# Rebuilding a state-space mixer: split f32r products of 128 columns between the chunk cores, and wider modulation strips

## The reference, cut to what matters

```
proj = h @ w_in                      # 1024 x (q k v f u_pool z xbc dt gates)
y_att  = forgetting_attention(q, k, v, log_sigmoid(f + b)) @ w_attn_o      # 16 heads of 64
y_pool = multiscale_pool(u_pool) by 4 windows, then 4 group products
# state-space branch: 4 groups of 8 heads of 64, state 128
xbc = silu(causal_depthwise_conv(xbc, 4 taps) + b);  xs, B, C = split(xbc)
dt = softplus(dt_raw + dt_bias);  a_cs = cumsum over the chunk of dt * -exp(a_log)
scores = (C B^T) * exp(a_cs[l] - a_cs[s]) * dt[s]  where l >= s
states = sum of B * exp(a_cs[end] - a_cs) * dt * xs, carried from chunk to chunk with exp(a_cs[end])
y = scores @ xs + (C @ states before the chunk) * exp(a_cs) + d_skip * xs
y = rms_norm_per_group(y * silu(z)) * norm_w;   y_ssm = y @ w_o
mix = (sigmoid(g0) * y_att + sigmoid(g1) * y_pool + sigmoid(g2) * y_ssm) @ w_out
```

## Time and profile before

| | us |
|---|---|
| median of 3 runs (3609.61 to 3610.5) | 3609.9 |
| profiled execution, its own time | 3614.2 |
| its span from first to last instruction | 3612.5 |
| TensorE busy | 2898.8 (80%) |
| VectorE busy | 1620.5 (45%) |
| ScalarE busy | 912.7 (25%) |
| mean granted TensorE clock | 0.877 of full speed |

### The profile page before, as it was taken

One profiled execution on the slowest core, in us unless ns is written; L12 is line 12 of the kernel. 1 busy time (PEld: TensorE's weight loads), 2 busy tenths in 40 slices (PEclk: granted clock), 3 DMA queues, 4 the chain that ended last, 5 costly groups with the idle time before them and its releaser, 6 DMA issues. The chain is left out here.

```text
span 3612.5 us, 34337 instructions
## 1 busy us (share of the span) xinstructions
PE 2898.8 (80%) x12461; PEld 1983.9 (55%) x12461; DVE 1620.5 (45%) x2729; ACT 912.7 (25%) x1385; POOL 48.3 (1%) x148
## 2 busy tenths in 40 slices
PE   3599878768998878839999558879998556879998
PEld 3366657524444456524444224458786556658786
DVE  7488843435566533421111244444334386344343
ACT  1333232212223232211111123333132212233132
POOL 0000000000000000010000100000000000000000
PEclk6798879879999989959999777889999758889999
DMA  8367531121110031028888400122230210222230
GB/s 305 88 206 211 173 117 47 59 61 57 58 35 23 0 117 46 25 72 318 316 318 319 151 28 15 54 81 94 86 100 12 60 26 24 71 93 94 86 100 23
DMA packets 301157, 376.39 MB, mean 104 GB/s; under 512 B 28072, under 2 KB 226203, under 8 KB 301052
## 3 DMA queue, kind: packets, MB, share of 16 engines
q1 hardware_dynamic: 293740, 349.28, 29.6%
q0 software_dynamic: 4000, 13.64, 1.0%
q10 hardware_dynamic: 3312, 12.06, 0.8%
HBM read 358.16 MB, written 16.79 MB: 104 GB/s over the span
## 5 line engine op out<-in xcount | busy, mean ns | idle before, releaser
L474 PE MATMUL banks<-mlp_h_parts,mlp_w_parts 128*128 128x512 f32 x1536 | 357.6, 396 | 58.1 <-DVE mlp_w_parts L462 58.1
L474 PEld LDWEIGHTS banks<-mlp_h_parts,mlp_w_parts 128*128 128x128 f32 x1536 | 294.1, 192 | 122.5 <-DVE mlp_w_parts L462 60.6
L474 PE MATMUL banks<-mlp_hidden,mlp_w_parts 128*128 128x512 f32 x1536 | 348.8, 389 | 0.0
L474 PEld LDWEIGHTS banks<-mlp_hidden,mlp_w_parts 128*128 128x128 f32 x1536 | 288.3, 188 | 59.9
L462 DVE TENSOR_TENSOR mlp_w_parts<-w_second,mlp_w_parts 128x2048 fp32r<-128x2048 f32 x64 | 146.5, 2292 | 208.7 <-ACT mlp_w_parts L457 208.7
L1849 PE MATMUL banks<-w,experts_xt 128*128 128x512 f32 x544 | 237.9, 595 | 0.9 <-DVE experts_xt L1900 0.9
L457 ACT ACTIVATE mlp_w_parts<-w_second 128x2048 fp32r<-128x2048 f32 x64 | 122.3, 1914 | 250.6 <-PE banks L474 245.8
L1849 PEld LDWEIGHTS banks<-w,experts_xt 128*128 128x128 f32 x544 | 103.9, 191 | 131.8 <-issue 131.8
L748 PE MATMUL banks<-h_parts,attention_w_parts 128*128 128x512 f32 x576 | 157.3, 427 | 18.0 <-DVE attention_w_parts L905 18.0
L947 DVE SCALAR_TENSOR_TENSOR attention_mod_sum<-w,silu_c,attention_mod_sum 128x256 f32<-128x256 f32 x336 | 162.8, 485 | 11.4
L1072 PE MATMUL banks<-h,w 128*128 128x512 f32 x384 | 165.9, 593 | 0.0
(11 more groups left out here) (577 smaller groups left out, 4321.4 us busy)
## 6 DMA issues: line engine op xcount, KB each, us to landing
w_second<-in_mlp_w_dram SPq DMA_DIRECT2D x64, 1024.0 KB, 5.3
w<-in_w_exp_gate_dram SPq DMA_DIRECT2D x17, 2048.0 KB, 9.4
w<-in_w_exp_up_dram SPq DMA_DIRECT2D x17, 2048.0 KB, 9.0
w<-in_w_exp_down_dram SPq DMA_DIRECT2D x17, 2048.0 KB, 11.0
w<-in_w_ada_dram SPq DMA_DIRECT2D x12, 2048.0 KB, 8.3
w<-in_mod_mix_w_dram SPq DMA_DIRECT2D x24, 1024.0 KB, 5.2
w<-in_mod_ffn_w_dram SPq DMA_DIRECT2D x24, 1024.0 KB, 5.1
w<-in_w_in_dram SPq DMA_DIRECT2D x32, 512.0 KB, 7.5
```

Source lines behind the costliest of these rows:

```text
L474: mm = pe.matmul(out, self.parts[:, n % 2, w, kk, f * P:(f + 1) * P], x[:, v, kk, :], start=(start and kk == 0 and j == 0), stop=(stop and ...
```

## The change

- `norm_in` no longer writes `k.h`: it scales in place in its own tile and keeps only the two parts `k.hp`, which now live until the end of the mixer. All products of h read them.
- `forget_stage` makes its 16 columns with a whole tile of 128 columns, split.
- In attention a modulation transfer is half the rows of a strip of 512 columns instead of all rows of 256. `matvec` makes 24 passes of 128 x 512 a pair instead of 48 of 128 x 256, and waits for its last pass at the end of each transfer.
- `merge_att` puts the branch output in a tile of its own and splits it at once. `merge_ssm` writes it over `k.hp` when its first phase is done, and reloads `k.x`.
- `ssm_stage` is rewritten. A list of 41 product tiles (dt for all 32 heads, then B, C, 4 of x, 4 of z for each group) of 128 columns: load (four raw buffers), high, low (two split buffers), 24 split products into one of two banks, eviction. The first eleven run ahead; the ten of group i+1 are placed between the steps of the chunk core of group i (`more(n)`). `k.x` is stored to DRAM at the start and its place used for work tiles. silu(v) is made as v/2 (1 + tanh(v/2)) with halved convolution weights. dt and a_cs are computed once for all 32 heads; a_cs is broadcast with two f32r products; the difference is an Abs activation with bias on ScalarE (four of 128 columns per head) ahead of exp(-|.|); x is weighted with dt out of PSUM; C B^T is masked once a group. `conv(t)` in the diff is a convolution, or for a z tile its gate, which reads the bank; the bank of `state(i, 2)` is emptied by the first pass of `states(i)`. The products of two heads alternate between the two halves of the output partitions.

The diff, cut to its core:

```diff
@@ norm_stage
+        dst = xc if dst is None else dst
@@ forget_stage
-        wf = sb("wf", [P, KD, HEADS])
+        raw, parts = sb("raw", [P, KD, P]), sb("parts", [P, 2, KD, P], F32R)
-            sp.dma_start(wf[:], columns(w_in, F0, HEADS)).then_inc(s["loaded"], 16)
+            sp.dma_start(raw[:], columns(w_in, F0, P)).then_inc(s["loaded"], 16)
@@ attention_stage, matvec
-                    j, kk = n // KD, n % KD
+                    j, kk = n // MOD_KD, n % KD
-                    acc, w, by = mod_sum[:, i % 2, j], mod_w[m % MOD_SLOTS][:, kk, :], k.silu_c[:, 1, kk:kk + 1]
+                    acc, w, by = mod_sum[:, i % 2, j // 2], mod_w[m % MOD_SLOTS][:, kk % MOD_KD, :], k.silu_c[:, 1, kk:kk + 1]
+                    if kk % MOD_KD == 0:
+                        dve.wait_ge(s[f"mod_loaded{m % MOD_SLOTS}"], 16 * (m // MOD_SLOTS + 1))
...
                         ins.then_inc(s["mod_used"], 1)
+                        dve.wait_ge(s["mod_used"], m + 1)
@@ ssm_stage, SyncE
+            load(0)
+            load(1)
+            sp.dma_start(k.x_store, k.x[:].rearrange("p k t -> p (k t)")).then_inc(s["x_stored"], 16)
             for half in range(2):
                 sp.dma_start(d_col[half * P_SSM:(half + 1) * P_SSM, :],
...
+            for t in range(2, TILES):
+                load(t)
@@ ssm_stage, TensorE
+            def tile(t):
+                pe.wait_ge(s["w_low"], t + 1)
+                if t >= 2:
+                    before = t - 2
+                    if before == 0:
+                        pe.wait_ge(s["dt_step"], 1)
+                    elif before in convs:
+                        pe.wait_ge(s["u_copied"], convs.index(before) + 1)
+                    else:
+                        pe.wait_ge(s["z_gated"], gates.index(before) + 1)
+                for kk in range(KD):
+                    for j, (w, x) in enumerate(((0, 0), (0, 1), (1, 0))):
+                        mm = pe.matmul(ps[:, t % 2, :], parts[:, t % SPLITS, w, kk, :], k.hp[:, x, kk, :], start=(kk == 0 and j == 0),
+                                       stop=(kk == KD - 1 and j == 2))
+                mm.then_inc(s["tile_done"], 1)
...
+            for i in range(G_SSM):
+                more(0)
+                turn_b(i)
+                turn_x(i, 0)
+                more(1)
+                turn_x(i, 1)
+                turn_x(i, 2)
+                more(2)
+                turn_x(i, 3)
+                chunk_products(i)
+                more(3)
+                state(i, 0)
+                state(i, 1)
+                state(i, 2)
+                rows(i, 0)
+                for f in range(KG):
+                    more(4 + f)
+                    heads(i, f)
+                    if f + 1 < KG:
+                        rows(i, f + 1)
+                more(8)
+                squares(i)
+                more(9)
@@ ssm_stage, ScalarE
+            def high(t):
+                if t < TILES:
+                    act.wait_ge(s[f"loaded{t % RAWS}"], 16 * (t // RAWS + 1))
+                    if t >= SPLITS:
+                        act.wait_ge(s["tile_done"], t - SPLITS + 1)
+                    act.activation(parts[:, t % SPLITS, 0], raw[:, t % RAWS], ACT.Copy).then_inc(s["w_high"], 1)
+            def tile(t):
+                high(t + 2)
+                if t >= 1:
+                    evict(t - 1)
+                if t >= 2:
+                    tanh(t - 2)
...
+            high(0)
+            high(1)
+            act.wait_ge(s["small_loaded"], 64)
+            act.activation(a_log[:], a_log[:], ACT.Exp).then_inc(s["a_ready"], 1)
@@ ssm_stage, VectorE
+            def tile(t):
+                low(t + 2)
+                if t >= 1:
+                    conv(t - 1)
+                if t >= 2:
+                    silu(t - 2)
+            for i in range(G_SSM):
+                more(0)
...
+                weigh(i, 0)
+                more(1)
+                weigh(i, 1)
+                weigh(i, 2)
+                more(2)
+                weigh(i, 3)
+                mask_products(i)
+                more(3)
+                states(i)
+                for f in range(KG):
+                    scores(i, f)
+                    more(4 + f)
+                    if f >= 1:
+                        outputs(i, f - 1)
+                more(8)
+                outputs(i, KG - 1)
+                normalise(i)
+                more(9)
@@ merge_stage
+        parts = k.hp if last else sb("x_parts", [P, 2, KD, T], F32R)
+            if last:
+                sp.dma_start(k.x[:].rearrange("p k t -> p (k t)"), k.x_store).then_inc(s["x_back"], 16)
+                sp.wait_ge(s["x_back"], 16)
```

More of the change, by code:

```diff
@@ L500, in _ @@
             for n in range(self.HALVES):
-                self.products(pe, n, self.x_parts, [k.ps[:, n * HT + f, :] for f in range(HT)], arriving=(n == 0))
+                self.products(pe, n, self.x_parts, [k.ps[:, n * HT + f, :] for f in range(HT)], arriving=(n == 0 and x is not None))
             if then:
@@ new lines, in squares, with more @@
+            def squares(i):
+                for f in range(KG):
+                    pe.wait_ge(s["sq_done"], KG * i + f + 1)
+                    mm = pe.matmul(ps[:, 2, :], k.ones[:], sq[:, f % 2, :], start=(f == 0), stop=(f == KG - 1))
+                    mm.then_inc(s["ms_done"], 1)
+            for t in range(1 + PER):
+                tile(t)
+                if t == 3:
+                    turn_small()
+            for i in range(G_SSM):
+                def more(n):
+                    if i + 1 < G_SSM:
+                        tile(1 + PER * (i + 1) + n)
+                more(0)
[20 more added lines that the diff above has]
+                more(9)
@@ new lines, in _, with more @@
+            for i in range(G_SSM):
+                def more(n):
+                    t = 1 + PER * (i + 1) + n
+                    if i + 1 < G_SSM:
+                        tile(t)
+                    elif n < 2:
+                        evict(t - 1)
+                        tanh(t - 2)
+                if i == 0:
+                    act.wait_ge(s["small_copied"], 3)
+                    act.wait_ge(s["x_stored"], 16)
+                more(0)
+                copy_b(i)
+                more(1)
+                more(2)
+                more(3)
+                for f in range(KG):
+                    exponents(i, f)
+                    more(4 + f)
+                    if f >= 1:
+                        square(i, f - 1)
+                more(8)
+                square(i, KG - 1)
+                root(i)
+                more(9)
@@ new lines, in _, with more @@
+            low(0)
+            low(1)
+            dve.wait_ge(s["small_loaded"], 64)
+            dve.wait_ge(s["a_ready"], 1)
+            for t in range(1 + PER):
+                tile(t)
+                if t == 1:
+                    times()
+                if t == 4:
+                    ends()
+            for i in range(G_SSM):
+                def more(n):
+                    t = 1 + PER * (i + 1) + n
+                    if i + 1 < G_SSM:
+                        tile(t)
+                    elif n < 2:
+                        conv(t - 1)
+                        silu(t - 2)
+                more(0)
+                if i == 0:
+                    dve.wait_ge(s["decay_done"], 3)
+                    dve.wait_ge(s["x_stored"], 16)
+                weigh(i, 0)
+                more(1)
+                weigh(i, 1)
+                weigh(i, 2)
+                more(2)
+                weigh(i, 3)
+                mask_products(i)
+                more(3)
+                states(i)
+                for f in range(KG):
+                    scores(i, f)
+                    more(4 + f)
+                    if f >= 1:
+                        outputs(i, f - 1)
+                more(8)
+                outputs(i, KG - 1)
+                normalise(i)
+                more(9)
@@ L1361, in _, with high @@
                     pe.wait_ge(s["gate_ready"], HT * (n % PER + 1))
[L1362 to L1363 removed]
+                mul.products(pe, n, k.hp if phase == 0 else parts, [ps[:, c, :] for c in tiles(n)], start=(phase <= 1),
+                             stop=(phase in (0, phases - 1)), arriving=(n % PER == 0 and phase > 0), arrived=KD * (phase - 1))
         @block.scalar
         def _(act):
[L1367 to L1371 removed]
+            def high(phase):
+                for kk in range(KD):
+                    act.activation(parts[:, 0, kk], x[:, (phase - 1) * KD + kk, :], ACT.Copy).then_inc(s["x_high"], 1)
             mul.high(act, 0)
             mul.high(act, 1)
+            if not last:
+                high(1)
             for n in range(N):
```

714 lines of the change are left out of this document (371 added, 343 removed).

## The result

The changed kernel takes 3548.2 us (median of 4 runs, 3543.2 to 3550.6) where the kernel before takes 3609.8 beside it: a ratio of 0.9824, with a 95% interval of 0.9812 to 0.9836. It is faster by 62 us; forecast were 92. A second comparison later gave 0.9816 (0.9802 to 0.9831). The profiled execution took 3550.6 us, its span 3548.8, so 63.7 less than the span before. The time lies in the outer range (3445 to 3585) and 3 us above the forecast's own (3490 to 3545).

A forecast was written before the change was run, and what follows sets the result against it. Bound taken: TensorE's state-space projections and chunk core follow one another. Terms -65 (that stage), -22 (attention), -7 (merge_att), +2.5 (forget) give -91.5: 3614.2 to 3522.7, less 4.3, 3518 us; range 3445 to 3585, forecast's own 3490 to 3545.

The forecast's parts named there:

- Forget, attention, merge_att: Three stages outside the state-space stage: forget 2.5 us slower, attention 22 us faster, merge_att 7 us faster.
- the prediction's own terms, 21 and 3: Attention: 21 us from three of four slices of a pair over seven periods, 3 more from the last pair.
- The start of the stage: State-space stage: small loads queue behind the store of x; tile 2 starts at 763.5, tile 10 ends at 839.
- The queues' order: State-space tiles: splits ahead of evictions make TensorE wait 1.9 us a tile, 3.3 for z tiles; pitches 7.6 and 9.0.
- One group, 105.5 us: State-space group with the next one's ten tiles inside: steps 96.8, with a table load 98, with four restarts 105.5 us.
- more(5) to more(9), where VectorE sets the pace: Second five tiles inside a group: VectorE's 10.5 us steps and a 6.4 us squares wait, together 48.7 us.
- about four a group, 1.9 each: State-space groups: waits of 3 to 5 us bring about four slow restarts of TensorE, 1.9 us each.
- The last group: State-space group without tiles beside it: 13.8 us to first heads, pair pitch 7.8, in all 49, with half clock 53.
- fall to 1.2 GHz for the stage: Rival, chance 0.08: waits drop TensorE's clock through the state-space stage, making it slower than before; 3688 with 33 slow tiles.
- No table is loaded between Exp and Tanh: Judges the longer-chain rival, chance 0.17: exponent/tanh table loads or slower hand-overs add 12 to 15 us a group, 3563.
- The waits hide better: Rival, chance 0.15: state-space groups run near TensorE's bound, 79 to 85 us each, giving 66 us more: 3452.
- the signs of being wrong: State-space stage: group pitch under 90 or over 120, tiles over 8 us, or table loads between Tanh and Exp.

The follow-up runs named there:

- experiment 1: Changed kernel with ScalarE evicting before its weight split and VectorE doing convolution or gate before its half of the split: 3473.6 us, ratio 0.9617.
- experiment 5: Changed kernel plus filling products that nothing reads in TensorE's longer waits of the start and first three groups, nothing moved: 3513.3 us, ratio 0.9730.
- experiment 7: Changed kernel with evictions first on both engines, small loads first, rows ahead of heads in the last group, and fewer fillers in remaining waits: 3452.5 us, ratio 0.9555.
- experiment 4: Changed kernel with evictions ahead of splits on both engines, and small loads and weights of tiles 2 and 3 ahead of x's store: 3456.9 us, ratio 0.9569.

## Why the prediction was right, and where 30 us went

- *Forget, attention, merge_att:* +2.7, -23.1 and -6.7 against +2.5, -22 and -7, and the last two also by taking them back. In attention that is partly luck. A wide pass kept VectorE for 0.75 us where 0.85 was assumed from the earlier trace rows, so a pair's passes fell by 5.2 us (22.4 to 17.2) and not by 4.0, while the period fell by 3.5 and not by three quarters of 5.2; and the prediction's own terms, 21 and 3, add up to 24 where it took 22.
- *The start of the stage:* right. The small loads wait behind the store and d_skip, tile 2 starts within a microsecond of the forecast, and from the stage's first transfer to the end of tile 10 are 110.8 us, forecast 111.6.
- *The queues' order:* right in mechanism and in size (1.78 and 3.15 for 1.9 and 3.3, 4.86 for 5, pitch 7.48 for 7.6; between z tiles 10.4 for 9.0 and a restart of 1.9), and experiment 1 shows that it was the dearest line of the change.
- *One group, 105.5 us, measured 110.3 on average:* two terms mis-sized. The step "more(5) to more(9), where VectorE sets the pace" gave 48.7 and a table load, 50; at full clock it is 54.3 on average (experiment 5). By the rows there VectorE does not set the pace alone but takes turns with ScalarE, whose square waits for `outputs` and holds back the next exponents; and a group has two table loads, at the Sqrt and at the Tanh behind it, where one was counted. The first half, 48.1, measured 47.5. The restarts, "about four a group, 1.9 each", cost 8.4 on average instead of 7.5. In single places they cost much more: the loss behind a wait was taken from 8 slow products, while a whole tile behind the longer waits took 8.5 us, 2.8 over its 5.7, and states, rows and heads between two waits ran slow as well. In all 3 x 4.8 = 14 us.
- *The last group:* 61.9 instead of 53, 9 us, and here the term at full clock failed, not the one for the clock. TensorE ran at 1.2 GHz through all four pairs (granted clock 0.50 from 1163 to 1193; the first four head products of a pair, eight records, take 1.12 us instead of 0.66). Fillers that hold the clock in the pairs take 5 us off, where 4 had been added for it. What is left is 56.9 for a forecast of 49: 18.3 us to the first heads instead of 13.8 (18.1 in experiment 7, at a granted clock of 1.00), a pitch of 8.68 instead of 7.8, and 12.6 from the last heads to the end instead of 11.8. Part of the pitch is the rows' place behind the heads: with rows first and fillers it is 7.67. The 18.3 us, the largest part of the miss, were not taken apart by any run (VectorE is busy for 13.9 of them).
- *The rest:* +1.8 between the starts of pool and pool_out, +4.2 and -2.3 behind the stage, none of it in the sum. Of the +4.2 most is spread; the other two stay open.

Together 14 + 9 = 23 of the 28 us between forecast (91.5) and traces (63.7); the rest is the last line of this list (3.7) and about a microsecond either way in the others.

The rivals: TensorE did not fall to 1.2 GHz for the stage (granted clock 0.88 to 0.91 in the groups, 0.63 only in the last core), but the clock behind each wait, on which that rival rests, cost 8.4 us a group and 5 in the last, of which the forecast had 7.5 and 4. No table is loaded between Exp and Tanh: the stage has four loads at Sqrt, three at the Tanh behind it and three at its start, 1.28 us each. By the rule of the Trainium skill (ScalarE: Activation LUTs, Table sets: the hidden batching unit) the two functions share a set; the trace agrees. "The waits hide better" did not come true of itself; experiment 4 reached its time (3457 us for 3452) by turning the queues and the loads, with groups of 90 to 92 us and not the 79 to 85 of that rival. `heads` takes its 14 products in 1.68 us (867.01 to 868.69) for a forecast of 1.9. Of the signs of being wrong, the pitch (under 90 or over 120) and the table loads did not show, and the one on tiles over 8 us did in five of 41.

## What to carry to other kernels

Where an engine both prepares the operand of a later tile and frees the bank of an earlier one, write the freeing first, on every engine of the chain: with one of two engines turned the wait only moved. A wait of TensorE is priced with the slow work behind it; products thrown away in the waits show in one run how much is the clock's, and where: here 24 of 25 us in the first halves of the three groups, and next to nothing where two other engines set the pace. Where two engines take turns, add the chain in order of dependence and not one engine's busy time.

## What was not expected

- Filling products without use took 33 us (0.9%) off a kernel in which nothing else moved, and raised the granted clock of the first group from 0.91 to 1.00. Where the waits were already short they gave nothing: 91.8 against 91.4 us a group.
- One instruction order in two queues was worth 73 us, more than the rebuild itself had gained with the other order (62).
- The same attention code took 313.6 to 319.4 us between executions. Differences of a few microseconds between two single traces of a stage are not to be explained.
